# Tokens 0 to 255: two query blocks in one attention turn, with the exponentials one turn behind the scores

## The reference, cut to what matters

```python
def block(args):                       # diff_attention, for each block of 128 queries
    q_blk, i = args
    s = jnp.einsum('bqhcd,bkhcd->bhcqk', q_blk, k).astype(jnp.float32) * scale
    s = jnp.where(causal_mask(i, S)[None, None, None], s, -jnp.inf)
    p = jax.nn.softmax(s, axis=-1)
    a = p[:, :, 0] - lam * p[:, :, 1]
    return jnp.einsum('bhqk,bkhe->bqhe', a.astype(v.dtype), v)
...
def block(args):                       # mla_attention
    qn, qr, i = args
    s = (jnp.einsum('bqhd,bkhd->bhqk', qn, k_nope)
         + jnp.einsum('bqhr,bkr->bhqk', qr, k_rope)).astype(jnp.float32) * scale
    s = jnp.where(causal_mask(i, S)[None, None], s, -jnp.inf)
    p = jax.nn.softmax(s, axis=-1)
    return jnp.einsum('bhqk,bkhe->bqhe', p.astype(v.dtype), v)
```

## Time and profile before

| | |
|---|---|
| median of 3 runs | 3197.68 us (3190.82 to 3199.83) |
| profiled execution | 3198.7 us, span of the trace 3196.9 us |
| granted TensorE clock, mean | 0.934 |
| busy | PE 86%, DVE 62%, ACT 45%, POOL 53% |

### The profile page before, as it was taken

The page is one execution under the profiler, slowest core; times in us unless marked ns, Lnnn a source line. Parts: engine busy times, 40 slices in busy tenths (PEclk is TensorE's granted clock), DMA queues, the critical chain, the costliest instruction groups (busy, mean ns, idle before and its releaser), DMA issues.

```text
span 3196.9 us, 43153 instructions
## 1 busy us (share of the span) xinstructions
PE 2742.5 (86%) x15358; PEld 2109.8 (66%) x15358; DVE 1981.3 (62%) x4201; ACT 1443.6 (45%) x3200; POOL 1679.2 (53%) x1014
## 2 busy tenths in 40 slices
PE   6986997798778878769889998869997999999998
PEld 3855896575333333238557776647876979998998
DVE  5676544467777777667677667767667373245323
ACT  2232222223333344345776555686555355444543
POOL 4813221283444444347437886528884607863685
PEclk8988998899999999979889998899998999999999
DMA  7210001227999999978979998889997505642453
GB/s 287 97 75 1 1 1 53 90 89 290 421 421 422 420 422 421 387 313 317 380 265 356 402 405 342 321 310 368 411 412 288 159 19 165 189 143 78 140 178 119
DMA packets 140516, 797.46 MB, mean 249 GB/s; under 512 B 15504, under 2 KB 18704, under 8 KB 67600
## 3 DMA queue, kind: packets, MB, share of 16 engines
q0 software_dynamic: 73728, 536.90, 41.4%
q1 hardware_dynamic: 65856, 253.36, 22.6%
q10 hardware_dynamic: 720, 4.46, 0.3%
HBM read 788.10 MB, written 6.55 MB: 249 GB/s over the span
## 4 chain that ended last, share of the span: by engine, by line
PE 44%; DMA 14%; DVE 14%; POOL 9%; issue 8%; ACT 6%; ACTq 0%; DVEq 0%; SPq 0%; POOLq 0%
PE ps L2528 7%; PE ps L1770 7%; PE ps L2547 7%; PE ps L879 6%; DMA raw<-in_peer_uv,un 5%; PE ps L1973 5%; POOL wls L302 4%; PE ps L332 3%; DVE scratch L1873 2%; POOL wlw L302 2%; DMA w<-in_peer_uv,un 2%; DMA raw<-in_peer_uv,scratch 2%; DMA un<-in_peer_uv,un 2%; DMA w<-in_peer_uv,scratch 1%; POOL raw L1751 1%
## 5 line engine op out<-in xcount | busy, mean ns | idle before, releaser
L302 POOL TENSOR_TENSOR wls<-raws,whs 128x1024 fp32r<-128x1024 f32 (+1 forms) x256 | 613.1, 2405 | 379.3 <-ACT whs L296 373.8
L1770 PE MATMUL ps<-raw,un 128*128 128x512 f32 x730 | 385.1, 646 | 110.5 <-ACT un L1831 110.1
L1824 ACT ACTIVATE un<-un 128x1 f32<-128x1 f32 x512 | 103.4, 202 | 599.2 <-DVE scratch L1873 581.5
L1973 PE MATMUL ps<-ts,whs 128*128 128x256 f32 x1424 | 303.9, 314 | 28.9 <-DVE ts L2068 19.3
L1751 POOL DMA_INDIRECT raw<-in_peer_uv,un x205 | 204.3, 997 | 210.4 <-PE ps L1770 129.7
L302 POOL TENSOR_TENSOR wlw<-raws,whw 128x1024 fp32r<-128x1024 f32 x112 | 267.8, 2407 | 75.5 <-ACT whw L296 74.7
L296 ACT CAST whs<-raws 128x1024 fp32r<-128x1024 f32 (+1 forms) x256 | 263.7, 1036 | 91.8 <-PE ps L2547 35.2
L1770 PEld LDWEIGHTS ps<-raw,un 128*128 128x128 f32 x730 | 133.2, 203 | 257.3 <-ACT un L1831 172.0
L1973 PEld LDWEIGHTS ps<-ts,whs 128*128 128x128 f32 x1424 | 241.6, 204 | 61.0 <-issue 36.9
L1873 DVE SCALAR_TENSOR_TENSOR scratch<-raw,ps 128x1024 f32<-128x1024 f32 x149 | 181.2, 1216 | 97.9 <-DMA raw<-in_peer_uv,un 88.2
L2547 PE MATMUL ps<-ts,whs 128*128 128x256 f32 x1216 | 240.2, 298 | 0.0
(11 more groups left out here) (445 smaller groups left out, 7177.9 us busy)
## 6 DMA issues: line engine op xcount, KB each, us to landing
raws<-in_w_up SPq DMA_DIRECT2D x128, 512.0 KB
raws<-in_w_down SPq DMA_DIRECT2D x128, 512.0 KB
scratch<-in_ada_w SPq DMA_DIRECT2D x17, 1024.0 KB, 13.5
raws<-in_w_qk SPq DMA_DIRECT2D x32, 512.0 KB
raw<-in_w_in SPq DMA_DIRECT2D x11, 1024.0 KB, 6.0
raw<-in_peer_w_q SPq DMA_DIRECT2D x8, 1024.0 KB, 8.0
raws<-in_w_v SPq DMA_DIRECT2D x16, 512.0 KB
raws<-in_w_o_a SPq DMA_DIRECT2D x16, 512.0 KB
```

Source lines behind the costliest of these rows:

```text
L302: e.tensor_tensor(self.wl[h][:, 0:width], self.raw[slot][:, 0:width], self.wh[h][:, 0:width].bitcast(F32), ALU.subtract).then_inc(*self.ti ...
L1770: ins = e.matmul(self.ps[:, b + half, :], self.diag[n % 4], self.rows[self.row_of(n)][:, 1024 + 512 * half:1536 + 512 * half], start=k == ...
L1824: e.activation(self.gelus[:, c], self.dots[:, c], ACT.Gelu, bias=0.0, scale=1.0).then_inc(*self.tick(S))
L1973: ins = e.matmul(o[:, 0:256], l, r, start=k == 0 and i == 0, stop=k == nk - 1 and i == 2)
```

## The change

For half 0 alone, `attention` gives way to `pairs`. A turn takes one head with both its query blocks. 8 heads are done in 11 turns, and each turn yields 2.4 in place of 1.2.

- Scores of both blocks lie in one bank (columns 0 to 127 the first, 128 to 383 the second), the transposes and the outputs too.
- DVE's scaled negatives and reciprocals are done for both blocks (and both maps) in one instruction. Maxima, exponentials and normalisations keep their number and width.
- ACT copies three transposed squares at once (128x384), and one output of 256 columns.
- On PE and DVE `scores` of head n are in turn n; on ACT `pairs` is called with `late=1`, so the exponentials of head n are in its turn n+1. On PE and ACT the transposes of head n stay in turn n+2 and its meet in turn n+3, on DVE its softmax is in turn n+2.
- The buffers of exponentials and transposes are used for two heads in turn.

```diff
+    def pairs(self, scores, softmaxed, turn, meet, late=0):
+        for n in range(11):
+            if 2 <= n <= 9:
+                softmaxed(n - 2)
+            if late <= n < 8 + late:
+                scores(n - late)
+            if 2 <= n <= 9:
+                turn(n - 2)
+            if n >= 3:
+                meet(n - 3)
+            yield 2.4
+    def pe_pair_turn(self, e, S, n, blocks, A_, D_):
+        o, before = self.slot((S, "turn", n), (A_, ("turn", n)))
+        for f in before:
+            e.wait_ge(*self.at(*f))
+        e.wait_ge(*self.at(D_, ("soft", n)))
+        for i, a in enumerate((blocks[0][:, 0:128], blocks[1][:, 0:128], blocks[1][:, 128:256])):
+            ins = e.transpose(o[:, 128 * i:128 * i + 128], a, self.C("ident"))
+        ins.then_inc(*self.tick(S, ("turn", n)))
+    def act_pair_turn(self, e, S, n, aT, P_):
+        if n >= 2:
+            e.wait_ge(*self.at(P_, ("meet", n - 2)))
+        e.wait_ge(*self.at(P_, ("turn", n)))
+        e.copy(aT, self.bh((P_, "turn", n), 384)).then_inc(*self.tick(S, ("turn", n)))
...
     def pe_diff(self, e, H):
+        def pair_scores(n):
+            for c in range(2):
+                p = slice(64 * c, 64 * c + 64)
+                o, freed = self.slot((S, "score", n, c), (A_, ("exp", n, c)))
+                for f in freed:
+                    e.wait_ge(*self.at(*f))
...
+                for qb in range(2):
+                    w, at = 128 * (qb + 1), 128 * qb
+                    e.matmul(o[:, at:at + w], H.q[p, n, 128 * qb:128 * qb + 128], H.k[p, n, 0:w], start=True, stop=False)
+                    ins = e.matmul(o[:, at + 128 * qb:at + w], self.C("ident"), self.C("causal"), start=False, stop=True)
+                ins.then_inc(*self.tick(S, ("score", n, c)))
...
+        if h:
+            yield from self.attention(H, scores, self.nothing, turn, meet)
+        else:
+            yield from self.pairs(pair_scores, self.nothing, pair_turn, pair_meet)
     def act_diff(self, e, H):
+        def pair_scores(n):
...
+            if n >= 2:
+                e.wait_ge(*self.at(P_, ("turn", n - 2)))
+            e.wait_ge(*self.at(D_, ("max", n)))
+            st = small[:, 104 + 16 * (n % 2):120 + 16 * (n % 2)]
+            for c in range(2):
+                for qb in range(2):
+                    w, at, i = 128 * (qb + 1), 128 * qb, 8 * c + 4 * qb
+                    e.activation(H.E[2 * (n % 2) + qb][:, 256 * c:256 * c + w],
+                                 self.bh((P_, "score", n, c), at + w)[:, at:at + w], ACT.Exp, bias=st[:, i + 1:i + 2], scale=0.125,
+                                 accum_out=st[:, i + 2:i + 3]).then_inc(*self.tick(S, ("exp", n, c) if qb else None))
...
+        if h:
+            yield from self.attention(H, scores, self.nothing, turn, meet)
+        else:
+            yield from self.pairs(pair_scores, self.nothing, pair_turn, pair_meet, 1)
     def dve_diff(self, e, H):
+        def pair_scores(n):
+            st = small[:, 104 + 16 * (n % 2):120 + 16 * (n % 2)].rearrange("p (g k) -> p g k", k=4)
+            for c in range(2):
+                e.wait_ge(*self.at(P_, ("score", n, c)))
+                for qb in range(2):
+                    w, at = 128 * (qb + 1), 128 * qb
+                    e.tensor_reduce(st[:, 2 * c + qb, 0:1], self.bh((P_, "score", n, c), at + w)[:, at:at + w], AX,
+                                    ALU.max).then_inc(*self.tick(S))
+            e.wait_ge(*self.last(S))
+            e.tensor_scalar(st[:, :, 1], st[:, :, 0], -0.125, None, ALU.mult).then_inc(*self.tick(S, ("max", n)))
...
```

More of the change, by code:

```diff
@@ L1934, in tail_tiles @@
             H.maT = [plain(f"mat{h}{i}", aT + wide * i, wide) for i in range(4)]
+            H.maT2 = [plain(f"map{h}{i}", aT + 512 * i, 384) for i in range(2)]
             H.mE = [plain(f"me{h}{i}", gel + wide * i, wide) for i in range(4)]
@@ L2163, in nothing, with pe_pair_meet @@
     @staticmethod
-    def nothing(n, hh, qb):
+    def nothing(*block):
         return None
+    def pairs(self, scores, softmaxed, turn, meet, late=0):
[22 more added lines that the diff above has]
+        e.copy(aT, self.bh((P_, "turn", n), 384)).then_inc(*self.tick(S, ("turn", n)))
+    def pe_pair_meet(self, e, S, n, v, aT, A_, freed):
+        o, before = self.slot((S, "meet", n), freed)
+        for f in before:
+            e.wait_ge(*self.at(*f))
+        e.wait_ge(*self.at(A_, ("turn", n)))
+        for q, kb in ((0, 0), (1, 0), (1, 1)):
+            c = 128 * (q + kb)
+            ins = e.matmul(o[:, 128 * q:128 * q + 128], v[:, kb, 128 * n:128 * n + 128], aT[:, c:c + 128], start=kb == 0,
+                           stop=kb == q)
+        ins.then_inc(*self.tick(S, ("meet", n)))
     def queries(self, H, qb):
@@ L2805, in meet, with pair_scores, pair_turn, pair_meet @@
                    self.bh((P_, "meet", n), 128)).then_inc(*self.tick(S, ("put", n)))
-        yield from self.attention(H, scores, self.nothing, turn, meet)
+        def pair_scores(n):
+            st = small[:, 104 + 8 * (n % 2):112 + 8 * (n % 2)]
+            if n >= 2:
+                e.wait_ge(*self.at(P_, ("turn", n - 2)))
+            e.wait_ge(*self.at(D_, ("max", n)))
+            for qb in range(2):
+                w, at = 128 * (qb + 1), 128 * qb
+                e.activation(H.mE[2 * (n % 2) + qb][:, 0:w], self.bh((P_, "score", n), at + w)[:, at:at + w], ACT.Exp,
+                             bias=st[:, 4 * qb + 1:4 * qb + 2], scale=192.0 ** -0.5,
+                             accum_out=st[:, 4 * qb + 2:4 * qb + 3]).then_inc(*self.tick(S, ("exp", n) if qb else None))
+        def pair_turn(n):
+            self.act_pair_turn(e, S, n, H.maT2[n % 2], P_)
+        def pair_meet(n):
+            e.wait_ge(*self.at(P_, ("meet", n)))
+            e.copy(H.A[n][0], self.bh((P_, "meet", n))).then_inc(*self.tick(S, ("put", n)))
+        if h:
+            yield from self.attention(H, scores, self.nothing, turn, meet)
+        else:
+            yield from self.pairs(pair_scores, self.nothing, pair_turn, pair_meet, 1)
         yield from self.act_residual(e, H, S, D_, P_, "w_o_b", self.gain("mlp_norm_g_2", 8))
```

93 lines of the change are left out of this document (87 added, 6 removed).

## The result

The changed kernel takes 3214.75 us (median of 5 runs, 3212.41 to 3222.43), against 3197.68 (3190.82 to 3199.90) for the kernel before: a ratio of 1.0062, 95% interval 1.0048 to 1.0075. It is slower by about 17 us, on the side and within the range that was forecast, 7 us under the forecast time.

The account below looks back on a forecast made before the run. ScalarE was taken to bound the attentions. Differential attention +16 - 4 + 5 = +17 and MLA +8 - 4 + 3 = +7 make +24 on 3198.7, 3222.7, so 3222 for the median; range 3194 to 3246, likeliest case 3208 to 3244.

Parts of the forecast that it names:

- Loads: Both attentions of half 0: 16 turns with exponentials become 8 in each, removing 20.5 us of table loads, 41 over both.
- The chain in the differential attention: ScalarE's copy waits for transposes queued behind scores that its own exponentials let go; +16 us for the 11 turns.
- The copy's wait: Differential attention: ScalarE's copy of the transposes waits for PE about 3 us in each of turns 4 to 8.
- the turns' 11.7 to 13.2: Differential attention: us from one Exp load to the next, 11.65 with two rows and 13.2 with three.
- the stretch: Differential attention from the first exponential load: 112 to 117 us, against 96 before.
- The clock: TensorE's lower clock level lengthens the turns: 5 us in the differential attention (share 0.38), 3 in MLA (share 0.2).
- The first and last turns: Differential attention: turn 0 takes 8 us, turn 8 with three rows 13.2, turns 9 and 10 8 and 5.8.
- the +16 at full clock: Differential attention: 11 turns take 112 us against 96 before, without the terms for rows and clock.
- MLA: one step was wrong: MLA attention: transposes wait behind the last row's product and next scores, ready at 3.4 us; 100 against 92 us, +8.
- Rows: Four more rows in each attention, eight fewer in MLP 1 of half 0, 0.94 us each: -8, -4 per attention.
- Rival 1: Both attentions: if banks come free before PE asks, the loads' time arrives, 31 us faster, 3167; chance 0.15.
- The draw: Chain overlaps partly: differential attention turns 10.8 to 11.5, MLA gains 1 to 2 us a turn; 3198 us, chance 0.22.

Follow-up runs that it names:

- before_noload: Kernel before, with Identity in place of Gelu in the rows' activation, so no table is changed for it: 3165.21 us, 0.9908.
- rows_by_two: Kernel before, with the rows of two turns of half 0's attentions issued behind the second, nothing paired: 3197.06 us, 0.9997.
- diff_only: Changed kernel with the change kept in the differential attention alone, MLA attention of half 0 as in the kernel before: 3225.11 us, 1.0091.
- rows25: Changed kernel, each of the 11 turns yielding 19 x 1.2 / 11 in place of 2.4, so 25 rows per attention, not 29: 3214.93 us, 1.0062.
- both_orders: Changed kernel, TensorE's scores put behind transposes and meet, and VectorE's maxima at the head of its turn, in both attentions: 3193.54 us, 0.9995.
- pe_order: Changed kernel, TensorE doing transposes and meet of a turn ahead of the scores, on its list alone: 3241.07 us, 1.0136.
- dve_order: Changed kernel, VectorE taking the maxima of head n at the head of its turn n+1, on its list alone: 3228.46 us, 1.0098.

## Why the prediction was right, point by point

- **Loads.** 32 fewer for exponentials and Gelus in the two attentions, each 1.28 us: as said. The next exponential starts 0.01 us behind the load (1598.21), and before_noload, without nearly all of the 64 that the two attentions had and without those of other rows, saves 30 us, less than the 82 of the 64. By the 2.66 us for each switch in the Trainium skill, "ScalarE: Activation LUTs", section "What ACT_TABLE_LOAD costs", these 64 would be 170 us, an estimate. This case's traces don't show the draining in it: the load of turn 5 starts 0.02 us behind the instruction ahead of it, and the exponential 0.01 us behind the load.
- **The chain in the differential attention.** Mechanism and order as written out: first bank free at 2.3 us, transposes behind both scores, copy, Gelu load, rows from VectorE's dot products. The two waits that were forecast are the two at the top of the list. The copy's wait was forecast as about 3 us, though the prediction's own times (asked for at 3.0, ready at 6.8) give 3.8; it was 6.7. And turns 4 to 7 took 15.0, 16.6, 16.3 and 14.0 where 11.65 and 13.2 were worked out at the full clock. So three of the numbers by which the prediction wanted to be known failed: the copy's 3 us, the turns' 11.7 to 13.2, and the stretch, 112 to 117 by forecast and 125.8 counted as there.
- **The clock is the term that was too small.** I took a share of 0.38 at the lower level and so 5 us in five turns (and wrote 3 for MLA, where 0.2 x 3 x 6 is 3.6). The scores' records of turn 5 are at the lower level (1.22, the one of the earlier trace rows), while a row's product later in the turn is back at the full one (1.08 for two at 1609.31, where two took 1.91 at 1607.60). The window from 1581.90 to 1643.75 has a mean of 0.67, but the mean is not what counts: in turn 5 the lower level lies just on the chain. Both scores end 9.0 us into the turn, where 6.05 was forecast. At 11.65 and 13.2, plus the full 2.6 in each, these four turns make 60.1; they took 61.9.
- **The first and last turns.** Turn 0 was given 8 us. Scores start at 1534.6 and the first exponentials' load comes at 1553.36, 18.8 us later, where before it was 4.4 and the turn: 14.4 for 8. ScalarE waits there 4.07 and 5.12 us for a row's dot product (1546.18 and 1552.32), and the DMA is at its full share (1.02, 410 GB/s) all the while. The turns from 8 on took 22 us for 28 (the forecast's 13.2, 8 and 5.8, and the 1 us by which the stage of the table ends later than the stretch of the forecast). Together with 1 us more in turns 1 to 3 and the 12.1 in turns 4 to 7 this is +6.4 +1 +12.1 -6, 13.6 us beside the +16 at full clock, and the stage's 29.8 in this run.
- **MLA: one step was wrong.** I let the last row's product and the scores of the next head stand ahead of the transposes within ScalarE's turn, with the transposes ready at 3.4 us and a turn of 9.2 and 11.0. The scores' bank doesn't wait there, so they run before the turn, and the transposes start 2.26 us into it, right behind the exponentials. The turns took 8.4 and 10.15. So +4.6 in place of +11 (8 and 3 for the clock), and a stage of 97.5 us where the stretch was forecast at 100 to 103.
- **Rows.** -6.3 against -8, so 0.8 us for each of eight rows where 0.94 was worked out and 1.3 held possible, but only with both attentions changed. The last row's diagonal starts 29.7 us ahead of the end of MLP 1 (2434.7, 2464.4), 7.6 before (2443.2, 2450.8): 22 us, at 3.8 us a row some six rows' worth where eight were said.
- **The middle stage** gave 5.7 us that nobody had forecast. Its instructions are the same. Among all profiled runs it lies between 404.7 and 416.1: 404.7 to 412.0 with both attentions paired, 413.5 to 416.1 in before and with one of them paired, but 407.8 and 409.0 in rows_by_two and before_noload, which pair nothing. As diff_only and after have the same instructions up to its end, a part of this varies by execution; what sets it stays open.

So +29.0 for +21, +4.6 for +11, -6.3 for -8, and the rest, -5.7 and what lies ahead of the attention, by no step of mine. The mechanism and the side of the result were forecast; that the time came within 7 us is luck, as two mis-sized terms of opposite sign and the unforecast stage make the total look better than its parts. Rival 1, the loads' time, fell: its condition (banks free before TensorE asks) does hold in the MLA attention, and there a turn is indeed 1.3 us shorter than before; four more rows in the stretch and its longer ends take that back (with the old number of rows, in rows25, 4.4 us of gain are left). The draw, in time, came true for both_orders, by another way than written: its turns of 8.1 and 10.1 us are shorter than the draw's 10.8 to 11.5.

What isn't settled: why halving the loads brings nothing in both_orders and rows_by_two, while taking all away brings 30 us. Both kernels have waits of their own. In the differential attention of both_orders the middle gained and the ends gave it back, and TensorE's transposes wait 17.7 us for VectorE there and 27.3 in the MLA attention, which at 94.7 us gained nothing. In rows_by_two ScalarE waits 15.2 us for maxima in the differential attention, and MLP 1 gives back what the MLA attention gained. No run takes one of these away alone.

## What to carry to other kernels

Before widening a step to save an engine's fixed cost, walk the new turn once over all engines: what frees the bank, who is queued behind the one who waits, and whether the waiting instruction's releaser lies in the same turn. If it does, the turn is a sum and no longer a maximum, and a reorder on one engine alone lengthens it (pe_order, dve_order); the queues have to be moved together. Price the links at the clock that the records on the chain show, not at the stretch's mean. And price the ends: here a turn twice as wide and a delay of one turn put the load for the first exponentials 18.8 us behind the first scores, where it was 4.4 before.

## What the runs showed of the hardware that was not expected

- The granted clock fell with the waits although TensorE's work grew: 0.81 to 0.73 in the differential attention. Within turn 7, TensorE was idle for 3.58 us, its first scores ran at the full level (2.4 GHz; 0.49 for two, at 1632.02), and those from 1634.31 on at the lower one (1.2 GHz):

```profile
1632.02 0.49 PE L2350 MATMUL ps<-k,q 64*128 64x128 f32 x2 [3.58 <-ACT e L2456]
...
1634.31 0.79 PE L2350 MATMUL ps<-k,q 64*128 64x128 f32 x2
```

- An exponential with a sum has a second record of its own, 0.19 to 0.21 us, which starts 0.1 us before the activation's end (1598.48, the exponential of 1598.21 lasting 0.37); the next exponential follows 0.1 us after that record's start (1598.57).
